# A bidirectional state space scan issued as one stream of 32 rounds instead of four groups of ten

## The reference, cut to what matters

```
def step(state, inp):                     # chunk of 128 tokens, group g, heads r
    xc, ac, bc, cc = inp
    acs = jnp.cumsum(ac, axis=1)
    seg = acs[:, :, None] - acs[:, None, :]
    decay = jnp.exp(jnp.where(lower, seg, -jnp.inf))
    cb = jnp.einsum('bign,bjgn->bijg', cc, bc)
    y_diag = jnp.einsum('bijg,bijgr,bjgrp->bigrp', cb, decay, xc)
    y_off = jnp.einsum('bign,bgrpn->bigrp', cc, state) * jnp.exp(acs)[..., None]
...
y = y_f + flip_seq(y_b) + xs * lp['d_skip'][:, None]
y = rms_norm_gated(y.reshape(b, l, D_INNER), z, lp['ssd_norm_g'])
```

## Time and profile before

| | |
|---|---|
| median of three runs | 3288.84 us (3288.74 to 3291.86) |
| the profiled execution, its own time | 3291.22 us |
| its span, first to last instruction | 3289.4 us |
| PE busy | 3038.2 us (92%) |
| DVE, ACT, POOL busy | 1379.4, 1072.6, 242.4 us |
| mean granted clock of PE | 0.953 of full |
| the scan, from its first transposes to u's first product | 209.57 to 401.57 us |
| u, z and gates | 401.57 to 529.3 us |

### The profile page before, as it was taken

How to read it: one execution, slowest core, us unless ns; L and a number is a source line. 1 busy time by engine, 2 the same in 40 slices (tenths; PEclk the granted TensorE clock), 3 DMA queues, 4 the chain that set the end, 5 groups by cost and what they waited for, 6 DMA issues and landing times.

```text
span 3289.4 us, 45808 instructions
## 1 busy us (share of the span) xinstructions
PE 3038.2 (92%) x19910; PEld 2353.2 (72%) x19910; DVE 1379.4 (42%) x2098; ACT 1072.6 (33%) x1580; POOL 242.4 (7%) x275
## 2 busy tenths in 40 slices
PE   6988899779999989999897888999999999898998
PEld 4866699755555547888676646888868887774898
DVE  4655554432222234333477354333343333436554
ACT  4433354222222223222342233322242222435443
POOL 0014470110000000000004000000000000200000
PEclk9988899979999999999999899999989999998999
DMA  7457754389999953232249221333222323310453
GB/s 229 155 181 229 247 157 138 107 320 389 391 393 392 391 232 112 81 115 69 79 137 307 88 77 52 99 93 104 77 88 90 103 88 102 131 65 1 141 182 101
DMA packets 415222, 537.41 MB, mean 163 GB/s; under 512 B 14340, under 2 KB 389924, under 8 KB 390308
## 3 DMA queue, kind: packets, MB, share of 16 engines
q1 hardware_dynamic: 415012, 534.38, 47.7%
HBM read 533.30 MB, written 1.05 MB: 162 GB/s over the span
## 4 chain that ended last, share of the span: by engine, by line
PE 82%; DVE 8%; ACT 5%; DMA 3%; issue 2%; SPq 0%; POOL 0%; DVEq 0%; ACTq 0%; POOLq 0%
PE ps L189 79%; PE ps L188 2%; DVE ar L244 2%; ACT ar L314 2%; DMA RAW<-in_ada_w 1%; DVE LR L244 1%; ACT HR L314 1%; DMA RAW<-in_w_in 1%; DVE ar L260 1%; DVE ar L250 1%; PE ps L195 1%; ACT arf1i L314 1%; DVE ar L263 1%; ACT L314 1%; DVE ar L254 1%
## 5 line engine op out<-in xcount | busy, mean ns | idle before, releaser
L189 PE MATMUL ps<-AH,HR 128*128 128x512 f32 (+1 forms) x2552 | 897.1, 352 | 45.6 <-DVE AL L244 18.4
L189 PE MATMUL ps<-AL,HR 128*128 128x512 f32 (+1 forms) x2552 | 888.4, 348 | 0.0
L189 PE MATMUL ps<-AH,LR 128*128 128x512 f32 (+1 forms) x2552 | 887.6, 348 | 0.0
L244 DVE TENSOR_TENSOR LR<-RAW,HR 128x2048 fp32r<-128x2048 f32 (+3 forms) x232 | 485.9, 2096 | 598.9 <-ACT HR L314 594.8
L314 ACT ACTIVATE HR<-RAW 128x2048 fp32r<-128x2048 f32 (+3 forms) x232 | 404.3, 1744 | 726.5 <-PE ps L189 628.5
L189 PEld LDWEIGHTS ps<-AH,HR 128*128 128x128 f32 x2552 | 492.4, 193 | 117.2 <-ACT AH L314 14.3
L189 PEld LDWEIGHTS ps<-AH,LR 128*128 128x128 f32 x2552 | 492.3, 193 | 59.0
L189 PEld LDWEIGHTS ps<-AL,HR 128*128 128x128 f32 x2552 | 492.8, 193 | 57.1
L189 PE MATMUL ps<-ar 64*128 64x128 f32 (+9 forms) x1318 | 238.6, 373 | 36.4 <-DVE ar L244 18.8
L244 POOL TENSOR_TENSOR ar<-ar 128x384 f32<-128x384 f32 (+5 forms) x138 | 153.0, 1117 | 1308.1 <-DMA ar<-in_cst 1024.0
L189 PEld LDWEIGHTS ps<-ar 64*128 64x128 f32 (+2 forms) x1318 | 140.4, 188 | 117.4 <-issue 46.6
(11 more groups left out here) (187 smaller groups left out, 3566.9 us busy)
## 6 DMA issues: line engine op xcount, KB each, us to landing
RAW<-in_ada_w SPq DMA_DIRECT2D x72, 1024.0 KB, 6.6
RAW<-in_f1i SPq DMA_DIRECT2D x44, 1024.0 KB, 5.1
RAW<-in_f2i SPq DMA_DIRECT2D x44, 1024.0 KB, 5.1
RAW<-in_w_in SPq DMA_DIRECT2D x32, 1024.0 KB, 5.7
RAW<-in_w_ada SPq DMA_DIRECT2D x24, 1024.0 KB, 8.2
RAW<-in_w_eu SPq DMA_DIRECT2D x17, 1024.0 KB, 9.9
HF<-in_w_ed SPq DMA_DIRECT2D x17, 1024.0 KB, 8.9
LF<-in_w_eu SPq DMA_DIRECT2D x17, 1024.0 KB, 10.1
```

The source lines that it names most:

```text
L189: return self.e.matmul(o, w, x, start=start, stop=stop)
L244: return self.e.tensor_tensor(o, a, b, op) if self.e else NOTHING
```

## The change

The four groups become one stream of 32 rounds (and two more for the products that lag). What prepares group g+1 is issued beside the last rounds of group g: on PE `rows(g+1)` after the products of round 5 and `states(g+1)` after those of round 7, `late_rows(g+1)` after the decays of the next group's round 0. DVE scales the context's rows in rounds 5 and 6, masks in round 0 and scales the latents' rows in rounds 0 and 1. `xd` gets a second set of buffers, `S0` one for each group, in memory that is free by then. The background steps are left out of the rounds for which `quiet` holds.

```diff
+ROUNDS = 32
+def quiet(R):
+    return R % 8 < 2 and R < ROUNDS or R % 8 > 4 and R < 24
 def ssd_pe(T, K):
+    T.hi = 6
     def products(n):
+        if n % 16 == 0:
+            T.wait_ge(*act.of("s0", g))
+            T.wait_ge(*dve.of("xdl", g))
...
-    for g in range(4):
+    def rows(g):
         turned(("bk", g), ...)
         for j in range(2):
             turned(("xc", g, j), ...)
+    def states(g):
         T.wait_ge(*dve.of("xdc", g))
         T.wait_ge(*act.of("bk", g))
...
+    def late_rows(g):
         for j in range(2):
             turned(("xl", g, j), ...)
-        T.wait_ge(*dve.of("xdl", g))
-        T.wait_ge(*act.of("s0", g))
-        T.hi = 6
-        for r in range(8 + LAG):
...
+    rows(0)
+    states(0)
+    for R in range(ROUNDS + LAG):
+        g, r = divmod(R, 8)
+        n = 2 * R
...
+        if R < ROUNDS and r == 0:
+            late_rows(g)
+        if not quiet(R):
             T.step()
-            if r >= LAG:
-                products(n - 2 * LAG)
-        T.hi = 8
+        if R >= LAG:
+            products(n - 2 * LAG)
+        if g < 3 and r == 5:
+            rows(g + 1)
+        if g < 3 and r == 7:
+            states(g + 1)
+    T.hi = 8
 def ssd_dve(V, K):
+    def masked(g):
         if g:
-            V.wait_ge(*pe.of("products", 16 * g - 1))
-        V.wait_ge(*dve.of("xbc end"))
-        scaled("xc", o.tokC, "xdc")
+            V.wait_ge(*pool.of("seg", 16 * g - 2))
+            V.wait_ge(*dve.of("seg", 16 * g - 1))
         V.wait_ge(*pe.of("cb", g, 0))
...
-        V.wait_ge(*pe.of("s0", g, 1))
-        scaled("xl", o.dtL, "xdl")
...
+        if not quiet(R):
             V.step()
...
+        if R < ROUNDS and r == 0:
+            masked(g)
+            V.wait_ge(*pe.of("s0", g, 1))
+        if R < ROUNDS and r < 2:
+            scaled("xl", o.dtL, "xdl", g, r)
+        if g < 3 and 5 <= r < 7:
+            if g and r == 5:
+                V.wait_ge(*pe.of("products", 16 * g - 1))
+            scaled("xc", o.tokC, "xdc", g + 1, r - 5)
```

More of the change, by code:

```diff
@@ L1136, in ssd_act @@
             K.free(act, "s0", g, d)
[L1138 to L1148, removed]
+    b_rows(0)
@@ new lines, in ssd_act @@
+    states(0)
+    for R in range(ROUNDS + LAG):
+        g, r = divmod(R, 8)
+        n = 2 * R
+        for x in (n, n + 1) if R < ROUNDS else ():
+            S.wait_ge(*pe.of("decay", x))
+            if x >= NB:
+                S.wait_ge(*pe.of("products", x - NB))
+            S.act(o.EC[x % NB], K.ps("decay", x)[:, 0:256], ACT.Exp).then_inc(*act("ec", x))
+            K.free(act, "decay", x)
+        for x in (n - 2, n - 1) if 1 <= R <= ROUNDS else ():
+            S.wait_ge(*dve.of("diff", x))
+            S.act(o.SEG[x % NB], o.SEG[x % NB], ACT.Exp).then_inc(*act("seg", x))
+        if not quiet(R):
@@ L1149, in ssd_act, with scaled @@
             S.step()
+        if g < 3 and r == 5:
+            b_rows(g + 1)
+        if g < 3 and r == 7:
+            states(g + 1)
     act.note("ssd end")
 def ssd_dve(V, K):
-    o, pe, dve, act = K.one, K.pe, K.dve, K.act
+    o, pe, dve, act, pool = K.one, K.pe, K.dve, K.act, K.pool
     V.wait_ge(K.loaded["tri"], 32)
[L1156 to L1164, removed]
+    def scaled(key, tok, done, g, j):
+        V.wait_ge(*pe.of(key, g, j))
+        src = K.ps(key, g, j)[:, :].rearrange("p (h c) -> p h c", h=8)
+        for d in range(2):
+            by = tok[:, j, 32 * d + 8 * g:32 * d + 8 * g + 8].unsqueeze(2).broadcast_to([128, 8, 64])
+            V.tt(o.xd[g % 2][d][j].rearrange("p (h c) -> p h c", h=8), src, by, MUL).then_inc(*dve(done, g))
+        K.free(dve, key, g, j)
@@ L1181, in ssd_dve @@
         K.free(dve, "cb", g, 1)
-        V.wait_ge(*pe.of("s0", g, 1))
-        scaled("xl", o.dtL, "xdl")
[L1184 to L1199, removed]
-            V.step()
[L1201 to L1206, removed]
@@ new lines, in ssd_dve @@
+    V.wait_ge(*dve.of("xbc end"))
+    for j in range(2):
+        scaled("xc", o.tokC, "xdc", 0, j)
+    for R in range(ROUNDS + LAG):
+        g, r = divmod(R, 8)
+        n = 2 * R
+        for x in (n, n + 1) if R < ROUNDS else ():
+            hh, d = o.item(x)
+            V.wait_ge(*act.of("ec", x))
+            if x >= NB:
+                V.wait_ge(*pe.of("products", x - NB))
+            for src, dst, j in o.parts(d):
+                V.ts(o.SEG[x % NB][:, dst], K.ps("decay", x)[:, src],
+                     o.tokL[:, j, 32 * d + hh:32 * d + hh + 1], 0.0, SUB, MIN).then_inc(*dve("diff", x))
+            K.free(dve, "decay", x)
+        for x in (n - 2, n - 1) if 1 <= R <= ROUNDS else ():
+            if o.item(x)[1] == 0:
+                V.wait_ge(*act.of("seg", x))
+                V.wait_ge(*dve.of("cb", x // 16))
+                V.tt(o.SEG[x % NB], o.SEG[x % NB], o.CB[:, 0, :], MUL).then_inc(*dve("seg", x))
+        if not quiet(R):
+            V.step()
+        if R > LAG and (R - LAG) % 2 == 1:
+            m = (n - 2 * LAG) // 4
+            V.wait_ge(*pe.of("products", 4 * m + 3))
+            V.stt(o.xsL[:, m, :], o.xsL[:, m, :], K.v("dskip", m), K.ps("y", m)[:, 0:256], MUL,
+                  ADD).then_inc(*dve("y", m))
+            K.free(dve, "y", m)
+        if R < ROUNDS and r == 0:
[7 more added lines that the diff above has]
+            scaled("xc", o.tokC, "xdc", g + 1, r - 5)
```

67 lines of the change are left out of this document (35 added, 32 removed).

## The result

| | before | after |
|---|---|---|
| median, beside each other on one chip | 3289.45 us (3288.74 to 3291.86) | 3374.79 us (3366.02 to 3379.4) |
| ratio, 95% interval | | 1.0256 (1.0236 to 1.0275): slower |
| span of the profiled execution, mean clock | 3289.4 us, 0.953 | 3372.6 us, 0.943 |

A forecast was written before the change was run, and what follows sets the result against it. PE was taken to bound the kernel (busy 92% of the span). Scan minus 32 and merge plus 85 give net +53 on 3291.2 us, 3344, less 2.4 for the median: 3342 us, range 3310 to 3370 (3288 to 3380 with other cases).

The forecast's parts named there:

- The scan, -32 forecast: Scan: head waits go and 22 of 40 background steps leave, so it takes 160.3 us against 192.0.
- the walk: Scan: one group followed in program order with the profile's durations; 25.8 us of PE work plus waits and clock, 35.
- The waits of round 1 (1.0) and round 2 (2.7): Scan, each group: PE's decays wait 1.0 us for banks freed by masks; round 2's step waits 2.7 for latents' scalings.
- The 4 us of a group set aside for the clock: Scan: 4 us added to each group's 30.8 at full clock, as idle time brings the lower clock level.
- u, +12 forecast: Stage u: every second entry waits, since its transfer's buffer is freed only by PE's background step; +12 us.
- z, +46 forecast: Stage z: landing, cuts, `yz`, square, sums and step form a 13.0 us turn against 7.1; eight entries, +46 us.
- Gates, +23 forecast: Gates: every second entry waits as in u, 8.8 us an entry for 5.8 before; 8 entries, +23 us.
- Behind gates, +4 forecast: `ya`, behind gates: two background steps and a wait between them, +4 us; later stages costed at nothing.
- The landing: Merge: 10.5 us from a transfer's issue to PE's start, between 10.1 by the ring rule and 10.9 in the trace.
- Rival 1: Merge: transfers land before they are needed, so merge costs 29 us; total -19, 3270 us, faster; chance 0.08.
- Rival 2: Scan: runs at POOL's pace, minus 83 us; with merge plus 85, 3291 us, the same; chance 0.08.
- Rival 3: Scan and merge: gaps bring the lower clock in most of both; scan -12, merge +105, 3382 us; chance 0.10.

## Why the prediction was right, and what it mis-sized

**What bounds the kernel.** Right: every us came and went on PE's stream or in its waits.

**The scan, -32 forecast, -27.4 measured.** A group took 31.9, 37.7 and 37.6 us (distance of the latents' transposes) for the 35 of the walk, and the last stretch 45.3 for 44. In the four other executions of the same scan, 160.3 to 163.6 us long, the second group took 34.5 to 34.6 us (by the context rows' transposes) and not 37.7, so the forecast's 160.3 is among what this scan takes, and the miss of 4 us shows no term that failed. The waits of round 1 (1.0) and round 2 (2.7) were found as one of 4.65 ahead of round 2's decays in groups 1 to 3. The walk had engine and cause right, but took the banks in strict turn: since `y` sends the others back to bank 0, the decays of round 2 already need the banks of the latents' rows. In group 0, where no `y` has moved the turn yet, the two waits stand where the walk had them (2.56 at the decays of round 1, 2.58 at the products of round 2's step), and so they do in group 1 of the run with banks in turn (2.39 and 1.86). Only their split was off: 4.3 to 5.1 us for 3.7. The 4 us of a group set aside for the clock were right in kind: PE's work of 25.8 us took 31.1.

**u, +12 forecast, +11.9 measured.** Right, by its mechanism: entries that wait for `LR` behind a transfer that waits for a step. That it fits to 0.1 us is luck: in the other runs with steps beside all of u it took 34.6 to 37.8 us.

**z, +46 forecast, +54.6 measured.** The loop was right link by link. From the issue to the start of `LR` it took 8.1 us in the mean of seven turns, as forecast. What was mis-sized is the step, costed at 1.33 at full clock. In the row shown it took 2.52, at the 1.2 GHz level, as the products in the earlier trace rows do; the eight took 17.6 us together and not 10.6, 7 us more. Beside it there is contention: in the first four entries, beside POOL's pooling, `LR` took 2.7 to 2.8 and `yz` 0.94, in the last four 2.29 and 0.42. That is 3.5 us in all over what was costed; the prediction named 3, by the Trainium skill ("SBUF — State Buffer", who interferes with whom), and left them out of its sum. The trace agrees with the rule: `LR` 2.81 with POOL's product at 2.65 beside it, against 2.29 and 0.74 apart.

**Gates, +23 forecast, +30.7 measured.** The waits are those forecast (four, 14.5 us). What was left out is the clock: PE is busy 63.9 us for 47.7 and eight steps of 1.33, 58.3; 5.6 of the 7.7 us are that.

**Behind gates, +4 forecast, +12.2 measured.** PE waits 3.6 us for `LR` in `ya`, which together with its two steps and its longer entries comes to 8.6. Of the last 3.6, some 3 arise between 714 and 1227 us of the kernel before, where the change edits nothing and the prediction costed nothing. The run without steps in merge is 2.2 us longer than before in much the same stretch (597.1 us for 594.9), so they are hardly the steps' doing; their cause stays open.

**The landing.** The prediction took 10.5 us from issue to PE's start rather than 10.1, since the one pair in the earlier trace rows took 6.47 to land. In z the first of a pair took 6.0 at the median and alone 5.6. The Trainium skill ("DMA: Bandwidth & Descriptors", section on queues, rings and completion order) says that descriptors are consumed in the order of their ring, by which the transfer behind should not hold up the first; the trace agrees nearly, with 0.4 us between the two. In the run with transfers of an eighth behind it the first took 5.6 us in z, and merge gave back 10 us, 0.5 for each of its 20 steps: the middle value taken was right.

**The rivals.** Rival 1 (transfers keep up) did not happen: PE waited for `LR` or the square in every turn of z, and did so with small transfers too. Rival 2 (the scan at POOL's pace, 109 us) did not happen: even with the banks in turn it takes 149.4. Rival 3 (the clock, 3382) was nearest in its number, and half of it was real: merge cost +109 as it had it (+105), the scan gained 27 and not 12. The term that was mis-sized is PE's work in merge, costed at full clock: 7 us of z and 5.6 of gates. The rows before had shown products at the lower level after idle stretches of 2 us, and the loop has a wait of 4 to 5 us in each turn.

## What to carry to other kernels

Work that fills an engine's waits costs less than its own length (1.06 us for a step of 1.33 here), and moved to a stage without waits it costs more, by the chain that it closes (3 to 7 us here): before a drain is removed, ask what is being done in it. When entries of one kind are put between entries of another in a shared ring, find out for each buffer who frees it and when; here a buffer freed by the last reader rather than by the first copy turned, by the order of the program, a look-ahead of two into one, and made a loop of issue, landing, cuts and reader. The loop is then walked link by link at the lower clock and with the neighbours' contention, since both come with it.

## What the runs showed of the hardware

- The same 1210 products of the scan kept PE busy for 120.6 us at a mean clock of 0.91 (28.8 us of idle time, in waits of at most 2.6 us but for one of 4.2 at its end) and for 133.2 at 0.81 (31.4 us, waits of up to 4.7): the lower clock cost more than the idle time did. Neither the longest wait nor the sum orders the clock by itself: the kernel before, with more products, had 23.1 us of idle time in waits of at most 2.5 us but for one of 4.1 at its end, and a clock of 0.82.
- An instruction of DVE with two inputs in SBUF and one of POOL slow one another both ways: DVE's `LR` from 2.29 to 2.81 us, POOL's product from 0.74 to 2.65 us in the same stretch.
- The second transfer of a pair of 1 MB issued 0.4 us apart lands 3.0 us behind the first (8.6 and 6.0 from their issues), while one alone takes 5.6.
